# A rebuilt prologue: pre_norm_g as one row spread by GpSimd, v weights in quarters, new orders on four engines

## What is computed

```python
h = rmsnorm(x, pre_g)                       # x * rsqrt(mean(x*x) + 1e-6) * pre_g
p = h @ w_in                                # 3328 columns
aq, ak, av, ag, bq, bk, bv, bg = split_projection(p)
ya = sliding_window_sink_attention(aq, ak, av, sinks) * silu(ag)
yb = differential_attention(bq, bk, bv, lam, lambda_init, subln_g) * silu(bg)
y = concatenate([ya, yb]) @ w_out
return x + rmsnorm(y, post_g)
```

## Time and profile before

| what | value |
|---|---|
| median of 3 runs | 531.47 us (531.39 to 532.06) |
| profiled execution | span 529.6 us, from its first to its last instruction; the answers give no separate time for it |
| PE busy | 511.7 us, 97% |
| DVE, ACT, POOL busy | 269.9, 250.5, 105.8 us |
| DMA | 32.57 MB, mean 61 GB/s |

### The profile page before, as it was taken

One profiled execution on the slowest core, in us unless ns is written; L12 is line 12 of the kernel. 1 busy time (PEld: TensorE's weight loads), 2 busy tenths in 40 slices (PEclk: granted clock), 3 DMA queues, 4 the chain that ended last, 5 costly groups with the idle time before them and its releaser, 6 DMA issues.

```text
span 529.6 us, 7514 instructions
## 1 busy us (share of the span) xinstructions
PE 511.7 (97%) x2776; PEld 424.8 (80%) x2776; DVE 269.9 (51%) x650; ACT 250.5 (47%) x614; POOL 105.8 (20%) x91
## 2 busy tenths in 40 slices
PE   6899999999999999999988999999999999999995
PEld 6799997888878887888875666678788887888884
DVE  3656002465675566445446687656555385443332
ACT  5454213466476466556565675644454463221211
POOL 3410303030112110212033243222201252000000
PEclk9999999999999999999999999999999999999998
DMA  8730005130101110110111010111000653332222
GB/s 295 228 123 2 1 15 143 41 74 6 40 10 33 40 41 0 41 40 9 34 41 27 14 41 1 40 41 41 0 1 0 144 176 120 102 132 84 80 79 79
DMA packets 41300, 32.57 MB, mean 61 GB/s; under 512 B 18544, under 2 KB 35888, under 8 KB 41264
## 3 DMA queue, kind: packets, MB, share of 16 engines
q1 hardware_dynamic: 38960, 27.89, 18.7%
q10 hardware_dynamic: 2304, 4.20, 2.1%
HBM read 27.40 MB, written 4.19 MB: 60 GB/s over the span
## 4 chain that ended last, share of the span: by engine, by line
PE 85%; ACT 4%; DVE 4%; issue 3%; DMA 2%; POOL 2%; SPq 0%; DVEq 0%; POOLq 0%; ACTq 0%
PE proj L1164 39%; PE scores L1263 14%; PE proj L1134 10%; PE scores L1183 7%; PE banks L1204 6%; PE banks L1194 3%; PE scores L1228 2%; PE banks L1246 2%; PE banks L1236 1%; PE scores L1107 1%; DVE k_stack L961 1%; DMA pre_g<-in_pre_norm_g 1%; DMA w_raw<-in_w_in 1%; ACT k_stack L762 1%; PE banks L1213 1%
## 5 line engine op out<-in xcount | busy, mean ns | idle before, releaser
L1164 PE MATMUL proj<-hT_hi,w_hi 128*128 128x512 f32 x336 | 90.0, 401 | 0.8 <-DVE k_stack L961 0.6
L1164 PE MATMUL proj<-hT_lo,w_hi 128*128 128x512 f32 x336 | 90.6, 402 | 0.0
L622 POOL TENSOR_TENSOR w_lo<-w_raw,w_hi 128x1024 fp32r<-128x1024 f32 x21 | 51.0, 2430 | 195.4 <-ACT w_hi L711 195.4
L1164 PE MATMUL proj<-hT_hi,w_lo 128*128 128x512 f32 x336 | 89.2, 400 | 0.0
L1164 PEld LDWEIGHTS proj<-hT_hi,w_hi 128*128 128x128 f32 x336 | 60.3, 188 | 15.0 <-issue 1.9
L1164 PEld LDWEIGHTS proj<-hT_hi,w_lo 128*128 128x128 f32 x336 | 60.8, 188 | 13.7 <-issue 1.9
L1164 PEld LDWEIGHTS proj<-hT_lo,w_hi 128*128 128x128 f32 x336 | 59.9, 188 | 13.2 <-issue 1.9
L1016 DVE CUSTOM_DVE_ANT_0 weights<-scores,dist_b 128x128 f32<-128x128 f32 (+7 forms) x64 | 45.9, 755 | 47.2 <-PE scores L1183 47.0
L782 ACT ACTIVATE weights<-weights,small 128x128 f32<-128x128 f32 (+7 forms) x64 | 49.0, 767 | 14.0 <-DVE small L1016 14.0
L792 ACT ACTIVATE weightsT<-banks 128x512 f32<-128x512 f32 (+3 forms) x48 | 23.5, 490 | 51.4 <-PE banks L1194 51.4
L1183 PE MATMUL scores<-k_stack,q_stack 128*128 128x512 f32 (+3 forms) x192 | 41.9, 353 | 0.0
(11 more groups left out here) (106 smaller groups left out, 724.7 us busy)
## 6 DMA issues: line engine op xcount, KB each, us to landing
w_raw<-in_w_in SPq DMA_DIRECT2D x13, 512.0 KB, 3.9
x_in<-in_x SPq DMA_DIRECT2D x8, 512.0 KB, 5.5
w_raw<-in_w_in SPq DMA_DIRECT2D x16, 256.0 KB, 3.6
x_res<-in_x SPq DMA_DIRECT2D x8, 512.0 KB, 4.4
out<-y_out ACTq DMA_DIRECT2D x16, 256.0 KB, 2.2
wv_raw<-in_w_in SPq DMA_DIRECT2D x2, 640.0 KB, 7.4
wo_early<-in_w_out SPq DMA_DIRECT2D x4, 256.0 KB, 4.5
w_raw<-in_w_out SPq DMA_DIRECT2D x4, 256.0 KB, 6.5
```

The lines of the kernel that those rows point to most:

```text
L622: nc.gpsimd.tensor_tensor(w_lo[:, n % SPLIT], w_raw[:, n % RAW], w_hi[:, n % SPLIT].bitcast(F32), ALU.subtract).then_inc(w_lo_ready, 1)
L1164: last = nc.tensor.matmul(to, w[:, slot, k, :], h[:, k, HALF * half:HALF * half + HALF], start=(p == 0 and k == first), stop=(p == PIECES ...
```

## The change

pre_norm_g is loaded as one row into partition 0 ahead of everything, and POOL spreads it over the partitions with `partition_broadcast`. The first group of v weights is loaded, copied and subtracted in four quarters of 2 feature blocks each; all `wv_lo` are made by DVE. Tile 1 is now cut in halves, too. The iotas move behind the last tile on POOL. ACT, DVE and PE get new orders. `project_v` no longer waits by itself; it makes one pass over some blocks, and the waits stand outside.

```diff
+    g_row = place("g_row", 192, [1, D_MODEL])
...
-        return [slice(0, KT // 2), slice(KT // 2, KT)] if t == 0 else [slice(0, KT)]
+        return [slice(0, KT // 2), slice(KT // 2, KT)] if t < 2 else [slice(0, KT)]
...
-            load_x(0)
-            sp.dma_start(pre_g[:, :], pre_norm_g[0:1, :].to_broadcast([P, D_MODEL])).then_inc(pre_g_loaded, 16)
-            for part in range(2):
-                k = slice(4 * part, 4 * part + 4)
-                sp.dma_start(wv_raw[:, k, 0:VG], w_cols[:, k, BV:BV + VG]).then_inc(wv_loaded[part], 16)
-            load_x(1)
-            load_x(2)
+            sp.dma_start(g_row[:, :], pre_norm_g[0:1, :]).then_inc(g_row_loaded, 16)
+            for t in range(3):
+                load_x(t)
+                if t == 2:
+                    break
+                for part in (2 * t, 2 * t + 1):
+                    k = slice(2 * part, 2 * part + 2)
+                    sp.dma_start(wv_raw[:, k, 0:VG], w_cols[:, k, BV:BV + VG]).then_inc(wv_loaded[part], 16)
             for i, (first, count, to) in enumerate(v_runs[1]):
+                load_x(3 + i)
                 sp.dma_start(wv_raw[:, :, to:to + count],
-                             w_cols[:, :, first:first + count]).then_inc(wv_loaded[2 + i], 16)
-                load_x(3 + i)
+                             w_cols[:, :, first:first + count]).then_inc(wv_loaded[4 + i], 16)
...
             pool.wait_ge(half_made, 1)
+            pool.wait_ge(g_row_loaded, 16)
+            nc.gpsimd.partition_broadcast(pre_g[:, :], g_row[:, :]).then_inc(pre_g_spread, 1)
             for t in range(TILES):
...
                 root(x_scale[:, t:t + 1], x_mean[:, t:t + 1], 1, x_scaled)
-                if t == 0:
-                    pool.wait_ge(wv_hi_ready, 1)
-                    k, cols = slice(0, 4), slice(0, VG)
-                    nc.gpsimd.tensor_tensor(wv_lo[:, k, cols], wv_raw[:, k, cols], wv_hi[:, k, cols].bitcast(F32),
-                                            ALU.subtract).then_inc(wv_lo_first, 1)
-                if t == 2:
...
             square_x(0)
+            high_wv(slice(0, 2), slice(0, VG), 0)
+            high_wv(slice(2, 4), slice(0, VG), 1)
             high_h(0, 0)
-            high_wv(slice(0, 4), slice(0, VG), 0)
             high_h(0, 1)
-            high_wv(slice(4, 8), slice(0, VG), 1)
             square_x(1)
+            high_wv(slice(4, 6), slice(0, VG), 2)
+            high_wv(slice(6, 8), slice(0, VG), 3)
+            high_h(1, 0)
+            high_h(1, 1)
+            square_x(2)
             for t in range(TILES):
+                store_v(t, 0)
+                if t + 3 < TILES:
+                    square_x(t + 3)
                 if t + 2 < TILES:
-                    square_x(t + 2)
-                if t + 1 < TILES:
-                    high_h(t + 1)
-                store_v(t, 0)
+                    high_h(t + 2)
...
             norm_x(0)
-            low_h(0)
-            low_wv(slice(4, 8), slice(0, VG), 1)
+            low_wv(slice(0, 2), slice(0, VG), 0)
+            low_h(0, 0)
+            low_h(0, 1)
+            low_wv(slice(2, 4), slice(0, VG), 1)
             norm_x(1)
-            for t in range(TILES):
-                if t + 2 < TILES:
-                    norm_x(t + 2)
-                if t + 1 < TILES:
-                    low_h(t + 1)
...
+            low_wv(slice(4, 6), slice(0, VG), 2)
+            low_h(1, 0)
+            low_h(1, 1)
+            low_wv(slice(6, 8), slice(0, VG), 3)
+            for t in range(2, TILES):
+                norm_x(t)
+                low_h(t)
+            low_wv(slice(0, 8), slice(VG, B_WIDTH), 4)
+            low_wv(slice(0, 8), slice(B_WIDTH, V_WIDTH), 5)
...
             turn_x(0)
+            ALL, EARLY, LATE = range(KT), range(KT // 2), range(KT // 2, KT)
+            pe.wait_ge(h_hi_ready, tile_count(0, 0))
+            pe.wait_ge(wv_hi_ready, 2)
+            project_v(0, 0, 0, EARLY, first=True)
+            for part in range(2):
+                pe.wait_ge(wv_lo_ready, part + 1)
+                if part:
+                    project_v(0, 0, 2, range(2, 4))
+                else:
+                    project_v(0, 0, 2, range(0, 2))
+                    pe.wait_ge(h_lo_ready, tile_count(0, 0))
+                    project_v(0, 0, 1, EARLY)
+            pe.wait_ge(h_hi_ready, tile_count(0))
+            for part in (2, 3):
+                pe.wait_ge(wv_hi_ready, part + 1)
+                project_v(0, 0, 0, range(2 * part, 2 * part + 2))
+            pe.wait_ge(h_lo_ready, tile_count(0))
+            project_v(0, 0, 1, LATE)
+            turn_x(1)
+            for part in range(2):
+                pe.wait_ge(h_hi_ready, tile_count(1, part))
+                project_v(1, 0, 0, LATE if part else EARLY, first=(part == 0))
+            for part in (2, 3):
+                pe.wait_ge(wv_lo_ready, part + 1)
+                project_v(0, 0, 2, range(2 * part, 2 * part + 2), last=(part == 3))
+            for t in range(1, TILES):
+                if t >= 2:
+                    wait_proj_free(pe, t)
+                    pe.wait_ge(h_hi_ready, tile_count(t))
+                    project_v(t, 0, 0, ALL, first=True)
+                    if t + 1 < TILES:
+                        turn_x(t + 1)
+                pe.wait_ge(h_lo_ready, tile_count(t))
+                project_v(t, 0, 1, ALL)
+                if t == 1:
+                    turn_x(2)
+                project_v(t, 0, 2, ALL, last=True)
+            pe.wait_ge(wv_hi_ready, 6)
...
```

More of the change, by code:

```diff
@@ L333, in hybrid_layer @@
     x_loaded = [sem(f"x_loaded{i}") for i in range(XS)]
-    wv_loaded = [sem(f"wv_loaded{i}") for i in range(4)]
+    wv_loaded = [sem(f"wv_loaded{i}") for i in range(6)]
     w_loaded = [sem(f"w_loaded{i}") for i in range(RAW)]
     wo_loaded = [sem(f"wo_loaded{i}") for i in range(WO_RAW)]
-    pre_g_loaded = sem("pre_g_loaded")
+    g_row_loaded = sem("g_row_loaded")
+    pre_g_spread = sem("pre_g_spread")
     post_g_loaded = sem("post_g_loaded")
@@ L358, in hybrid_layer @@
     wv_hi_ready = sem("wv_hi_ready")
-    wv_lo_first = sem("wv_lo_first")
     wv_lo_ready = sem("wv_lo_ready")
@@ L431, in feature_parts @@
     def feature_parts(t):
-        return [slice(0, KT // 2), slice(KT // 2, KT)] if t == 0 else [slice(0, KT)]
+        return [slice(0, KT // 2), slice(KT // 2, KT)] if t < 2 else [slice(0, KT)]
     def tile_count(t, part=None):
-        return t + 2 if t or part is None else part + 1
+        before = sum(len(feature_parts(m)) for m in range(t))
+        return before + (len(feature_parts(t)) if part is None else part + 1)
     def halves_done(kind, index, half):
@@ L639, in _ @@
                 root(x_scale[:, t:t + 1], x_mean[:, t:t + 1], 1, x_scaled)
-                if t == 0:
-                    pool.wait_ge(wv_hi_ready, 1)
-                    k, cols = slice(0, 4), slice(0, VG)
-                    nc.gpsimd.tensor_tensor(wv_lo[:, k, cols], wv_raw[:, k, cols], wv_hi[:, k, cols].bitcast(F32),
-                                            ALU.subtract).then_inc(wv_lo_first, 1)
-                if t == 2:
[L647 to L653, removed]
+            nc.gpsimd.iota(dist_b[:, :], [[-1, SEQ]], base=SEQ - P, channel_multiplier=1,
+                           allow_small_or_imprecise_dtypes=True).then_inc(dist_made, 1)
+            nc.gpsimd.iota(dist_a[:, 1, :], [[-1, P]], base=CHUNK, channel_multiplier=1,
+                           allow_small_or_imprecise_dtypes=True).then_inc(dist_made, 1)
+            for n in (0, 1):
+                low_weights(n)
             for step, *i in SCHEDULE:
@@ L864, in norm_x @@
                 if t == 0:
-                    dve.wait_ge(pre_g_loaded, 16)
+                    dve.wait_ge(pre_g_spread, 1)
                 dve.wait_ge(x_scaled, t + 1)
@@ L871, in norm_x, with low_h @@
                                                    ALU.mult).then_inc(x_normed, 1)
-            def low_h(t):
+            def low_h(t, part=0):
                 tokens = slice(P * t, P * t + P)
[L875 to L878, removed]
+                k = feature_parts(t)[part]
+                dve.wait_ge(h_hi_ready, tile_count(t, part))
+                nc.vector.tensor_tensor(hT_lo[:, k, tokens], x_turned_at(t)[:, k],
+                                        hT_hi[:, k, tokens].bitcast(F32), ALU.subtract).then_inc(h_lo_ready, 1)
             def low_wv(k, cols, part):
@@ L1109, in turn_x, with project_v @@
                     last.then_inc(x_turned, 1)
-            def project_v(t, g):
+            V_PASSES = ((hT_hi, wv_hi), (hT_lo, wv_hi), (hT_hi, wv_lo))
+            def project_v(t, g, p, ks, first=False, last=False):
                 n = TILES * g + t
-                wait_proj_free(pe, n)
-                pe.wait_ge(h_hi_ready, tile_count(t, 0))
+                h, w = V_PASSES[p]
                 tokens, cols = slice(P * t, P * t + P), slice(VG * g, VG * (g + 1))
[L1116 to L1136, removed]
+                for k in ks:
```

(12 more changed lines are left out.)

8 lines of the change are left out of this document (2 added, 6 removed).

## The result

The changed kernel took 547.37 us (median of 4 runs, 546.58 to 547.66) against 531.52 for the kernel before on the same chip: ratio 1.0294, 95% interval 1.0281 to 1.0307. It is 15.9 us slower, where no measurable change was forecast.

A forecast was written before the change was run, and what follows sets the result against it. TensorE, 97% busy, was taken as the bound, with 6.0 us of prologue idle winnable. Lead 2.55 less 2.48 given back made 0.1 us, 0.2 after correction, from median 531.47: 531.3, range 530.1 to 532.9.

The forecast's parts named there:

- g row and spread: Prologue: row lands at 3.8, GpSimd's spread takes 1.2 and ends at 5.0, before GpSimd is wanted at 5.8; no cost.
- a slack of 0.8: Prologue, GpSimd: time between the spread's expected end at 5.0 and the mean of tile 0 at 5.8.
- Rival 2: First multiply and first scale wait for a late spread: 1.8 us lost (533.1) or 3.7 (535.0); chance 0.11.
- The Trainium skill's rule: First call of a freshly loaded GpSimd kernel pays about 6 us for its code, unseen in profiles; about 536.6.
- The chances: Faster by more than 1.06 us 0.19, slower by more 0.18, within 0.63; forecast band 530.1 to 532.5 had 0.67.
- the old copy was just hidden by x 0: Prologue: removing pre_norm_g's 128-fold copy gains nothing, as the multiply also needs the scale, ready at 6.6; start was 6.51.
- the lead given back in the steady tiles: v projection: 2.55 us gained by transposes of tile 2, 2.48 lost again to TensorE stalls from tile 2 on.
- a ring of 4.72 us: Steady tiles: transposes, ScalarE's copy, low part, multiply, walked as 4.65 per tile against TensorE's 4.39; 0.26 idle each.
- Rival 1: Steady tiles: transposes 3 to 7 find input ready, so 2.3 us of stalls are won, 529.0; chance 0.15.
- Rival 3: Tiles 1 and 2: small operations still collide with VectorE's subtractions, up to 0.8 each, two give 532.9; chance 0.07 beyond forecast.
- The new load thus buys nothing here: Prologue: the row's load in place of the copy gives no earlier first multiply, 6.6 against 6.51.
- a shift there reaches the end unchanged: Behind the v projection: later work hangs on its end, so any prologue gain or loss passes whole to the end.

The follow-up runs named there:

- the shuffle kernel: Changed kernel with the pre_norm_g row loaded into four partitions and spread by a VectorE shuffle instead of GpSimd; 532.03 us, ratio 1.0007 to the kernel before.
- the pairs above: 128-fold DMA copy against VectorE shuffle, both on the changed kernel: 533.07 against 532.03 us; with VectorE's multiply ahead of the low part: 530.24 against 529.69.
- the copy kernel: Changed kernel with the 128-fold DMA copy of pre_norm_g behind x 0 in place of row and spread, new orders kept; 533.07 us, ratio 1.0028.
- the shuffle kernels: Kernels where VectorE's shuffle spreads the row: changed kernel with it 532.03 us, also with VectorE's multiply ahead 529.69; kernel before with it 531.34.
- the spread alone: Kernel before with only the pre_norm_g copy replaced by one row and GpSimd's spread, old orders and halves kept; 547.16 us in one execution.
- the copy with the multiply ahead: Changed kernel with the 128-fold DMA copy for the spread, and VectorE multiplying tile t+1 ahead of the low part of tile t; 530.24 us, ratio 0.9982.
- the row from ScalarE: Changed kernel with VectorE's shuffle and multiply ahead, the row's DMA issued by ScalarE ahead of square 0 instead of by SyncE; 530.99 us, ratio 1.0000.

## Why the prediction was wrong

The step that failed is **g row and spread**, "So it costs nothing, hidden by x 0's load and square". The first multiply, which the prediction put at 6.6 and named as a sign of being wrong if it came after 7, came at 20.14. The two terms that I could size from rows were fine: the row landed at 2.1 (taken 3.8; the shortest load of 512 KB was no lower bound for 4 KB), the operation took 1.30 (taken 1.2, bounds 0.99 and 2.42). What had no row, and stood at nothing in the sum, was the change of library, 8.8 us after the row's landing and 6.9 us behind the spread, against a slack of 0.8. Both ends of my range for this term came from operations of the library that is already loaded.

**Rival 2** had the place right (the spread ahead of the first scale on GpSimd) and carried 0.11. Its prices, 1.8 and 3.7 us, were too small by 14 and 12. The Trainium skill's rule beside it ("GPSIMD Engine Reference", "Instruction dispatch": about 6 us for the first call of a freshly loaded kernel, with no visible instruction) gave an estimate of 536.6. The runs agree with it for one way on idle queues, 5.49 and 5.75 us. Three things made it 15.7: the way back costs as much and is paid by whatever comes next; the change is slower beside loads; and both lie ahead of the one thing that the whole prologue waits for. I argued against it with the first iota's 0.99 us without a gap. That row showed only that the iota needs no change of library.

**The chances** were wrong with it: a loss of any kind had 0.18, and nothing above 532.9 was in the range, although the only new kind of operation in the diff had no row in the trace. The case by the Trainium skill's rule, 5 us of loss, belonged at least inside the range.

**Right, and shown** by the shuffle kernel, which has the change without the library: the old copy was just hidden by x 0 (first multiply 6.38, walked 6.6, before 6.51); matmuls from 8.72 (walked 8.9); transposes of tile 2 at 17.91 (walked 18.2, before 18.39); the lead given back in the steady tiles, with a ring of 4.72 us (walked 4.65); v projection until 76.66 (walked 76.3 to 76.7, before 76.62). Its 532.03 stands 0.4 above the kernel before's 531.65 with an interval that holds no change, and inside the forecast's 530.1 to 532.5. Rival 1 (the lead stays) is refuted for the order as written, and its price of 2.3 us is what the multiply's place then brought. Rival 3 did not happen at its size: the mean of tile 1 took 0.23 to 0.50 us in the kernels with the new orders, in place of 1.32. "The new load thus buys nothing here" holds for the first multiply, but not for the whole: without the copy ahead of them the quarters came earlier, which the pairs above put at 0.5 to 1.0 us.

**Wrong by a small amount**: "a shift there reaches the end unchanged". Behind the v projection 0.8 us were added. There is a pause before VectorE's first q_stack (issue 0.46 in the chain), which the copy kernel shows too (0.47) and the shuffle kernels do not. It does not account for all: the shuffle kernel and the spread alone have no such pause and still take 453.4 and 453.5 there, against 453.0 before. The cause was not tried.

## What to carry to other kernels

Before a GpSimd operation of a new kind goes into a kernel, look in the built program for the reload that comes with it, and count two changes of library, one for it and one for the next ordinary operation; together 13 to 19 us in these runs, free only where GpSimd has that long to spare. A trace can't price an operation that isn't in it, so a diff's only new kind of operation should have the widest range of all, and be tried alone first. And when an order lets TensorE run ahead, check the ring that feeds it: here the same lead was worth 2.3 us or nothing, by which of two instructions VectorE issued first.

## What the runs showed of the hardware that I had not expected

- GpSimd's change to library 1 takes longer beside the kernel's own loads: 5.49 and 5.75 us on idle queues, 9.2 to 10.5 beside nearly 3 MB. That code and loads share a path is the likely reason, and is not shown. One execution with all loads held back until the spread was done took 2.3 us less than the changed kernel (545.1 against 547.37).
- A shuffle on VectorE spreads 1024 floats from four partitions to 128 in 1.30 us, the same as GpSimd's spread, with no silence on any engine around it; clearing the tile took VectorE another 0.91 us while it was idle.
- A lone 4 KB load landed 1.4 us after its issue, while one of the same content to four partitions, issued from ScalarE beside x 0 and two quarters (1.15 MB), was used 4.2 us after its issue.
- The granted clock was at the 1.2 GHz level for 3.4 us from near 10 us in three kernels (the copy, the copy with the multiply ahead, the row from ScalarE), whose longest idle times before it were 1.18, 1.19 and 1.80 us, and stayed at 2.4 GHz in the two with the new orders and the shuffle from SyncE, and in the two with the old orders, which stood idle for 1.40 (the copy) and 1.27 (the shuffle) there. So the length of one idle time does not decide it; what does was not tried.
